# Padded weight slots and reversed token order in the weight passes of a four-layer trunk

## What is computed

```python
def _swiglu(h, w_gate, w_up, w_down):
    return (jax.nn.silu(h @ w_gate) * (h @ w_up)) @ w_down
...
    for i in range(DEPTH):
        x = x + 0.5 * _swiglu(_rms_norm(x, norm_ffn1[i]), ffn1_w_gate[i], ffn1_w_up[i], ffn1_w_down[i])
        h = _rms_norm(x, norm_mix[i])
        kind = i % N_MIXERS
...
        x = x + y
        x = x + 0.5 * _swiglu(_rms_norm(x, norm_ffn2[i]), ffn2_w_gate[i], ffn2_w_up[i], ffn2_w_down[i])
    return x
```

## Time and profile before

| | |
|---|---|
| median of 3 runs | 1987.56 us (1984.85 to 1987.9) |
| span of the profiled execution, first to last instruction | 1984.6 us |
| a device time of the profiled execution apart from its span | none is given; the runs lie 0.3 to 3.3 us above the span |
| TensorE busy | 1955.5 us, 99% |
| VectorE busy | 1420.7 us, 72% |
| ScalarE busy | 1044.4 us, 53% |
| mean granted TensorE clock | 0.997 of full speed |
| moved by DMA | 350.14 MB, mean 176 GB/s |

### The profile page before, as it was taken

How to read it: one execution, slowest core, us unless ns; L and a number is a source line. 1 busy time by engine, 2 the same in 40 slices (tenths; PEclk the granted TensorE clock), 3 DMA queues, 4 the chain that set the end, 5 groups by cost and what they waited for, 6 DMA issues and landing times.

```text
span 1984.6 us, 29082 instructions
## 1 busy us (share of the span) xinstructions
PE 1955.5 (99%) x12574; PEld 1717.6 (87%) x12574; DVE 1420.7 (72%) x1645; ACT 1044.4 (53%) x1250; POOL 101.6 (5%) x114
## 2 busy tenths in 40 slices
PE   7999999999999998999999999999999999999999
PEld 6888889888888896988888888788888888888887
DVE  7776678875787565877587658887758765778763
ACT  6554566554555344654465455575436544566542
POOL 3000001000200001100100000010000000001000
PEclk9999999999999998999999999999999999999999
DMA  7655434655665683665656553356566655435653
GB/s 238 194 183 182 149 128 154 192 188 189 192 191 180 201 249 83 191 191 182 200 191 192 177 184 128 107 176 191 183 196 190 191 183 180 148 128 171 191 189 107
DMA packets 336365, 350.14 MB, mean 176 GB/s; under 512 B 10077, under 2 KB 331886, under 8 KB 336238
## 3 DMA queue, kind: packets, MB, share of 16 engines
q1 hardware_dynamic: 331742, 343.58, 54.1%
q10 hardware_dynamic: 4496, 4.70, 1.2%
HBM read 346.04 MB, written 2.22 MB: 175 GB/s over the span
## 4 chain that ended last, share of the span: by engine, by line
PE 94%; DVE 3%; ACT 2%; issue 1%; POOL 1%; DMA 0%; ACTq 0%; DVEq 0%; POOLq 0%
PE banks L1443 49%; PE banks L1448 24%; PE banks L1434 5%; PE banks L1436 5%; PE banks L1435 5%; PE banks L1901 1%; PE banks L1660 1%; PE banks L1713 1%; ACT sb_w_high L470 1%; DVE sb_w_low L808 1%; PE banks L1680 1%; PE banks L1697 1%; ACT sb_scores L598 0%; PE banks L1818 0%; PE banks L1667 0%
## 5 line engine op out<-in xcount | busy, mean ns | idle before, releaser
L808 DVE TENSOR_TENSOR sb_w_low<-sb_raw,sb_w_high 128x2048 fp32r<-128x2048 f32 (+1 forms) x332 | 749.5, 2262 | 208.8 <-ACT sb_w_high L470 208.2
L1443 PE MATMUL banks<-sb_x_both,sb_w_high 128*128 128x512 f32 x2816 | 721.9, 393 | 1.9 <-ACT sb_w_high L470 1.9
L470 ACT ACTIVATE sb_w_high<-sb_raw 128x2048 fp32r<-128x2048 f32 (+1 forms) x332 | 618.5, 1867 | 122.2 <-DMA sb_raw<-in_ffn_w_down 109.0
L1443 PEld LDWEIGHTS banks<-sb_x_both,sb_w_high 128*128 128x128 f32 x2816 | 500.2, 189 | 82.2 <-ACT sb_w_high L470 2.3
L1448 PEld LDWEIGHTS banks<-sb_x_both,sb_w_low 128*128 128x128 f32 x2792 | 386.5, 188 | 35.2
L1448 PE MATMUL banks<-sb_x_both,sb_w_low 128*128 128x256 f32 x2792 | 394.6, 279 | 0.0
L1443 PE MATMUL banks<-sb_h_both,sb_w_high 128*128 128x512 f32 x1408 | 360.2, 395 | 0.0
L1443 PEld LDWEIGHTS banks<-sb_h_both,sb_w_high 128*128 128x128 f32 x1408 | 250.8, 188 | 45.3
L1448 PEld LDWEIGHTS banks<-sb_h_both,sb_w_low 128*128 128x128 f32 x1408 | 190.9, 188 | 16.9
L1448 PE MATMUL banks<-sb_h_both,sb_w_low 128*128 128x256 f32 x1408 | 194.4, 279 | 0.0
L488 ACT ACTIVATE sb_x_both<-sb_xT,sb_vec 128x256 fp32r<-128x256 f32 x96 | 43.3, 501 | 200.8 <-DVE sb_xT L841 176.1
(11 more groups left out here) (229 smaller groups left out, 1936.6 us busy)
## 6 DMA issues: line engine op xcount, KB each, us to landing
sb_raw<-in_ffn_w_gate SPq DMA_DIRECT2D x88, 1024.0 KB, 5.4
sb_raw<-in_ffn_w_up SPq DMA_DIRECT2D x88, 1024.0 KB, 5.3
sb_raw<-in_ffn_w_down SPq DMA_DIRECT2D x64, 1024.0 KB, 5.0
sb_raw<-in_ffn_w_down SPq DMA_DIRECT2D x32, 768.0 KB, 4.3
sb_raw<-in_fox_w_in SPq DMA_DIRECT2D x24, 1024.0 KB, 5.2
sb_raw<-in_conv_w_pw SPq DMA_DIRECT2D x12, 1024.0 KB, 5.4
sb_raw<-in_diff_w_in SPq DMA_DIRECT2D x12, 1024.0 KB, 5.0
sb_raw<-in_fox_w_out SPq DMA_DIRECT2D x8, 1024.0 KB, 4.8
```

The costliest lines, as they stand in the source:

```text
L470: act.activation(slot(w_high, b)[:, 0:width(b)], slot(raw, b)[:, 0:width(b)], ACT.Copy).then_inc(S["high_ready"], 1)
L808: dve.tensor_tensor(slot(w_low, b)[:, 0:width(b)], slot(raw, b)[:, 0:width(b)], slot(w_high, b)[:, 0:width(b)].bitcast(F32), ALU.subtract) ...
L1443: return pe.matmul(pair(bank[at][:, :]), high[:, n * P:(n + 1) * P], m_both, start=first, stop=last, skip_group_check=True)
```

## The change

Each slot of the rings gets 16 more values (64 bytes) that nothing reads or writes, so that slot s starts 64 s bytes further on than before; all tiles behind the rings move by 640 bytes. And the matmuls of the weight passes get their streamed operand and their sums with a step of -1: the last token is read first and its sum is written first. The values, their places and their order of accumulation over k stay. The loaded 128 x 128 tile isn't reversed.

```diff
@@ -33,6 +33,7 @@
 RING = 5
+SLOT = 2048 + 16
 FF_TILES = D_FF // P
@@ -78,9 +79,9 @@
-            raw = landing.enter_context(nc.sbuf_tensor("sb_raw", [P, RING, 2048], F32))
-        w_low = sb("w_low", [P, RING, 2048], F32R)
-        w_high = sb("w_high", [P, RING, 2048], F32R)
+            raw = landing.enter_context(nc.sbuf_tensor("sb_raw", [P, RING, SLOT], F32))
+        w_low = sb("w_low", [P, RING, SLOT], F32R)
+        w_high = sb("w_high", [P, RING, SLOT], F32R)
@@ -219,7 +220,7 @@
         def slot(t, b):
-            return t[:, b % RING, :]
+            return t[:, b % RING, 0:2048]
@@ -1431,6 +1432,7 @@
             def three_passes(dst, s_high, s_low, m_high, m_low, first, last, loose=False):
+                dst, m_high, m_low = dst[:, ::-1], m_high[:, ::-1], m_low[:, ::-1]
                 pe.matmul(dst, s_high, m_high, start=first, stop=False, skip_group_check=loose)
...
@@ -1440,12 +1442,12 @@
-                return pe.matmul(pair(bank[at][:, :]), high[:, n * P:(n + 1) * P], m_both,
+                return pe.matmul(pair(bank[at][:, :])[:, :, ::-1], high[:, n * P:(n + 1) * P], m_both[:, :, ::-1],
                                  start=first, stop=last, skip_group_check=True)
...
-                pe.matmul(bank[at][:, SEQ:2 * SEQ], low[:, n * P:(n + 1) * P], m_high,
+                pe.matmul(bank[at][:, SEQ:2 * SEQ][:, ::-1], low[:, n * P:(n + 1) * P], m_high[:, ::-1],
                           start=False, stop=False, skip_group_check=True)
```

## The result

The changed kernel takes 2019.19 us (median of 4 runs, 2017.99 to 2020.94) against 1987.3 us (4 runs) before: 1.0164 times as long, 95% interval 1.0149 to 1.0178. I forecast 1967 us, faster; it became slower by 32 us. The span of its profiled execution is 2018.0 us, 33.4 us above that of before.

The account below looks back on a forecast made before the run. The prediction took TensorE's own matmul pace, 1793 us of the 1984.6 us span, as the bound. Pad and reversal at the trace's best levels gave -20 us, other engines nothing: 1967 us from 1987.6, range 1942 to 1983.

Parts of the forecast that it names:

- What bounds the kernel: Whole kernel: only the pace of TensorE's own matmuls matters; those the change touches make 1793 us, 90% of the span.
- What is late next, and the other engines: After a TensorE gain: VectorE and DMA take the 0.1 us shorter pair; nothing is given back, even at 134 us.
- The pad's price for ScalarE and VectorE: Copies and subtractions on the ring slots: blocks stay in one run, so price nothing, covered by TensorE's matmuls.
- The pad: TensorE's weight passes: five slots give five offsets to each operand; between 20 us gained and 24 us lost.
- The reversal: Weight-pass matmuls with step -1: gain up to 134 us, loss up to 1659; nearest rows taken, -20 to +24 us.
- the sum: Whole kernel: -20 us, best levels of the trace throughout; span 1984.6 becomes 1965, median 1987.6 becomes 1967 us.
- room below (134 us): Full-pace matmuls: time beyond one column per period at 2.4 GHz, all that better reading could give back.
- rival A: Full-pace matmuls: excess belongs to streaming 4-byte values, not two reads meeting; nothing happens, 1984 to 1992 us; chance 0.14.
- B: Weight passes: reversed streams meet weight loads at less lucky offsets; +24 us, 2012, or twice that, 2036; chance 0.28.
- C: All 11,328 matmuls: backward step not at full pace, same jump in all slots; +57 us, 2044, or 3600; chance 0.08.
- D: Weight passes: operand and weight load run one way, most excess goes; half gone 1920 us, all 1854; chance 0.14.
- Where a matmul's streamed operand and the weight tile for the next one are read side by side: TensorE's full-pace matmuls: supposed origin of the 134 us excess, making it depend on the reads' offset and direction.

Follow-up runs that it names:

- The bursts: Kernel before plus bursts of 24 matmuls behind its end, varying offset, direction, columns and weight tile; 256 columns forward at 113.3 to 120.0 ns, backward 117.7 to 120.0.
- the layout that I chose by them: Kernel before, forward, no pad, `h_both` moved to +64 bytes from the weights, `w_low` and `w_high` set 128 bytes further apart: 1982.72 us against 1986.47 (0.9982).

## Why the prediction was wrong

**What bounds the kernel: right.** TensorE's pace set the end before and after; its busy time grew by 31.4 us and the span by 33.4. **What is late next, and the other engines: right.** No wait of weight appeared, only one of 0.4 us on a subtraction. The pad's price for ScalarE and VectorE was nothing, as said. One reading was wrong without consequence: the longest wait of a weight pass before wasn't the 1.9 us but one of 5.4 us, of L1434 on `sb_o_low`, and it is 5.4 us after as well.

**The pad: the size was in the bounds, the end was badly chosen.** I put it at -20 to +24 us and took -20. Alone it cost 17.7. The bursts suggest why. For the offsets of slots 1, 2, 3, 4 and 0 to `x_both` (64, 0, 192, 128 and 128 bytes modulo 256) they have 228.9, 226.7, 233.3, 232.2 and 232.2 ns at 512 columns, and the pad alone shows these levels slot by slot to about 1 ns but for the second tile of slot 2. Over the four offsets, 512 columns forward take 230.3 ns on average and 256 columns 117.5, so a couple takes 347.7, against 344.4 and 348.8 of before. That makes 2816 x 3.3 - 1408 x 1.1 + 2880 x 2.2 = 9.3 - 1.5 + 6.3 = 14 us (an estimate). The couples on `x_both`, two thirds of all, already stood below that mean, and spreading the slots over all offsets could only draw them to it.

**The reversal: its bounds were wrong.** "The same lines' own levels, -20 to +24 us", were the nearest rows, but they are all rows of forward reads. Backward alone cost 34.4 us, beyond the upper end, since it has no fast level: in the bursts it goes at forward's worst for 512 columns (233.3 ns) and at 117.7 to 120.0 for 256.

**The step that failed** is the sum: "I take -20 us, the best levels of the trace throughout", because there was "more room below (134 us)" and "five offsets make it unlikely that all tiles settle again on the slow levels". All tiles did settle on the slow levels, and not for want of offsets, but because the direction takes the offset's effect away, wholly at 512 columns and nearly so at 256. The room below wasn't there either. No burst, forward or backward, went under 113.3 ns for 256 columns or 226.7 for 512; both are 17/16 of the column-per-period times of 106.7 and 213.3. Of the 134 us that I counted as excess, the part up to that floor, 2816 x 20.0 + 1408 x 20.0 + 2880 x 6.7 = 104 us, was in every run, which is what rival A held of the excess. At most about 30 us depended on offset. Whether the floor is the stream's own isn't shown: no burst ran without loading a weight tile for each matmul.

**The rivals.** B's time, 2012 to 2036, holds the result, and its point of decision, a mean couple above 345 to 349 ns, is passed at 352 to 353. That fit of the time is luck: B's cause, less lucky places, costs 17.7 us with the pad alone and nothing measurable with a backward read. In the kernel after, half of the mark that I had set for C is seen, a jump in all slots alike. C's cause holds for the read and fails for the sums. Its 5 ns on each of 11,328 matmuls were 33.4 us / 11,328 = 2.9 ns. Nor is the jump the same for all: `h_both`'s couples rose by about 4 ns and `x_both`'s by 7.8, to one common level. D is excluded for the streamed operand; both reads reversed wasn't tried.

**"Where a matmul's streamed operand and the weight tile for the next one are read side by side": half shown.** For it: moving either one by 64 bytes moves the level, in the bursts and, for the weight tile, slot by slot with the pad alone. Against a simple form of it: one weight column stands at the same slowest and fastest levels as 128, the difference of the two offsets doesn't settle the level, and one burst has two levels. The Trainium skill's two independent read ports (page "TensorE: Matmul & The Clock Gate", section "Part 2: What happens when you issue a matmul") don't explain that a moved weight tile takes the stream from 113.3 to 120.0 ns. Why reading backward has only slow levels stays open.

## What to carry to other kernels

Where a kernel sits on one of several levels, find out first which one: a change that spreads it over all of them draws it to about their mean (here 14 us estimated, 17.7 measured), and a tuned layout can be better than that. Rows of the ordinary direction don't bound a step that the trace doesn't contain, so such a step needs a range that is open upward, however near those rows seem. And a burst of 24 equal matmuls behind the kernel's own work shows in one run which levels a disputed form has. It doesn't price a mixture: the 512-column levels carried over to the kernel (228.9 and 233.3 ns against 228.8 and 232.5), the 256-column ones only in part, and the layout that I chose by them missed its time.

## What the runs showed of the hardware

- No stream of float32r operands here went under 17/16 of a period per column at the 2.4 GHz level (113.3 ns for 256 columns, 226.7 for 512), however few weight columns were loaded.
- The level above it depends on where the streamed operand and the weight tile lie: 113.3 to 120.0 ns for 256 columns, where moving the streamed operand by 256 bytes changes nothing, and 226.7 to 233.3 for 512, with another best offset.
- A streamed operand read with a step of -1 stands at 233.3 ns for 512 columns at the four offsets tried. Sums written with a step of -1 cost nothing that can be measured (ratio 1.0001).
- The same 24 matmuls with 32 weight columns at the same offset took 2.96 us in one kernel and 2.82 in another, where only the bursts differ. What selects the level is open.
